# Four Strassen pairs of eight instead of three in gate and up, with the first weight sum made by accumulating DMA loads

## What is computed

```python
def _swiglu(h, w_gate, w_up, w_down):
    return (jax.nn.silu(h @ w_gate) * (h @ w_up)) @ w_down

x = x + _swiglu(_rmsnorm(x, ffn_norm[i]), ffn_w_gate[i], ffn_w_up[i], ffn_w_down[i])
```

## Time and profile before

| | |
|---|---|
| median of 3 runs | 2114.09 us (2113.99 to 2115.06) |
| the profiled execution: time, span | 2114.07 us, 2112.3 us |
| granted TensorE clock, mean | 0.998 |
| busy share PE, DVE, ACT, POOL | 99%, 82%, 56%, 1% |
| share of the chain that ended last: PE, DVE | 97%, 2% |
| DMA | mean 190 GB/s, the loads' queue 59.3% of the 16 engines |

### The profile page before, as it was taken

The page is one execution under the profiler, slowest core; times in us unless marked ns, Lnnn a source line. Parts: engine busy times, 40 slices in busy tenths (PEclk is TensorE's granted clock), DMA queues, the critical chain, the costliest instruction groups (busy, mean ns, idle before and its releaser), DMA issues.

```text
span 2112.3 us, 27946 instructions
## 1 busy us (share of the span) xinstructions
PE 2095.8 (99%) x9741; PEld 1743.9 (83%) x9741; DVE 1728.6 (82%) x1965; ACT 1179.5 (56%) x1321; POOL 15.4 (1%) x14
## 2 busy tenths in 40 slices
PE   8999999999999999999999999999999999999999
PEld 7888878888888888888878888888888888888887
DVE  5887757999999997877788788569999999978776
ACT  5466555665666654455455555555656565545443
POOL 0001000000000000000000000000000000000000
PEclk9999999999999999999999999999999999999999
DMA  7545555665666566666656665656665666566664
GB/s 229 156 139 154 173 169 176 199 208 189 199 199 207 190 198 200 199 198 192 191 183 191 186 201 186 199 178 198 201 200 188 200 200 200 193 204 196 206 198 132
DMA packets 234765, 401.63 MB, mean 190 GB/s; under 512 B 15040, under 2 KB 56128, under 8 KB 234688
## 3 DMA queue, kind: packets, MB, share of 16 engines
q1 hardware_dynamic: 233824, 399.23, 59.3%
q10 hardware_dynamic: 864, 1.37, 0.2%
HBM read 398.45 MB, written 2.10 MB: 190 GB/s over the span
## 4 chain that ended last, share of the span: by engine, by line
PE 97%; DVE 2%; ACT 0%; issue 0%; DMA 0%; SPq 0%; ACTq 0%; DVEq 0%
PE ps L767 24%; PE ps L769 24%; PE ps L768 24%; PE ps L513 6%; PE ps L544 4%; PE ps L542 4%; PE ps L543 4%; PE ps L518 3%; PE ps L577 2%; DVE w_lo L1354 0%; PE ps L695 0%; PE ps L633 0%; PE ps L704 0%; PE ps L685 0%; DMA res<-in_x 0%
## 5 line engine op out<-in xcount | busy, mean ns | idle before, releaser
L986 ACT ACTIVATE w_hi<-stage 128x1024 fp32r<-128x1024 f32 x748 | 782.0, 1057 | 755.4 <-PE ps L769 343.9
L1354 DVE TENSOR_TENSOR w_lo<-stage,w_hi 128x1024 fp32r<-128x1024 f32 x748 | 893.6, 1220 | 224.5 <-ACT w_hi L986 218.3
L767 PE MATMUL ps<-w_hi,xs 128*128 128x512 f32 x1254 | 491.0, 392 | 2.6 <-DVE w_lo L1354 2.6
L769 PE MATMUL ps<-w_hi,xs 128*128 128x512 f32 x1254 | 488.7, 390 | 0.0
L768 PE MATMUL ps<-w_lo,xs 128*128 128x512 f32 x1254 | 488.4, 389 | 0.0
L767 PEld LDWEIGHTS ps<-w_hi,xs 128*128 128x128 f32 x1254 | 235.7, 188 | 51.0 <-issue 3.0
L769 PEld LDWEIGHTS ps<-w_hi,xs 128*128 128x128 f32 x1254 | 235.6, 188 | 49.3
L768 PEld LDWEIGHTS ps<-w_lo,xs 128*128 128x128 f32 x1254 | 235.8, 188 | 48.1
L767 PE MATMUL ps<-w_hi,hs 128*128 128x512 f32 x584 | 227.6, 390 | 0.0
L769 PE MATMUL ps<-w_hi,hs 128*128 128x512 f32 x584 | 227.2, 389 | 0.0
L768 PE MATMUL ps<-w_lo,hs 128*128 128x512 f32 x584 | 227.2, 389 | 0.0
(11 more groups left out here) (209 smaller groups left out, 2480.9 us busy)
## 6 DMA issues: line engine op xcount, KB each, us to landing
stage<-in_w_gate SPq DMA_DIRECT2D x176, 512.0 KB, 3.7
stage<-in_w_up SPq DMA_DIRECT2D x176, 512.0 KB, 4.3
stage<-in_w_down SPq DMA_DIRECT2D x176, 512.0 KB, 4.5
stage<-in_conv_w_in SPq DMA_DIRECT2D x96, 512.0 KB, 4.3
stage<-in_attn_w_in SPq DMA_DIRECT2D x48, 512.0 KB, 3.7
stage<-in_attn_w_out SPq DMA_DIRECT2D x32, 512.0 KB, 5.2
stage<-in_conv_w_out SPq DMA_DIRECT2D x32, 512.0 KB, 4.8
stage<-in_attn_w_in SPq DMA_DIRECT2D x32, 256.0 KB, 3.2
```

Of the source, the lines that this page charges most:

```text
L767: pe.matmul(ps[:, bank, :], hi, b_hi, start=start, stop=False)
L769: return pe.matmul(ps[:, bank, :], lo, b_hi, start=False, stop=stop)
L986: nc.scalar.activation(w_hi[:, j % RING, :], stage[:, at, :], ACT.Copy).then_inc(hi_done, 1)
L1354: tt(w_lo[:, p, :], stage[:, stage_at(first + j), :], f32(w_hi[:, p, :]), ALU.subtract).then_inc(lo_done, 1)
```

## The change

- Gate and up have four mixed pairs in ten of the eleven units, 2, 3, 5 and 6; the last unit has 2 and 5. Pairs 2 and 3 and pairs 5 and 6 are neighbours. `sx` has four places.
- The signs of the scheme are turned so that the first sum of weights is b11 + b12. GpSimd makes it: a DMA from HBM that adds b11 (128 x 512, 256 KB) onto b12 in the odd slot in `stage` (`add_b11`), after that slot's load has landed and after the last such DMA has landed. The semaphore is `u1_added`. This holds for all mixed pairs, those of `down` and of the convolution too.
- `mix_weights` is two operations: one on 128 x 512 and one on 128 x 1024 that makes the other two sums with a repeated second operand. It waits for `t_ready` of the last pair (`t_raw` read), not for `t_used`.
- `mixed_high` and `mixed_low` are two operations each, 512 and 1024 columns. The wait for TensorE stands on ScalarE: the first copy waits for P6 of the last mixed pair, the second for P7.
- The convolution's third forms are made after slot 21 instead of slot 11.
- `P7` and `P5` change sign, in `take_mixed` and in the forms.

```diff
-        MIXED_PAIRS = (2, 4, 6)
-        LAST_MIXED = (2, 6)
-        FORM_PLACE = {4: 0, 2: 1, 6: 2}
+        MIXED_PAIRS = (2, 3, 5, 6)
+        LAST_MIXED = (2, 5)
+        FORM_PLACE = {3: 0, 6: 1, 2: 2, 5: 3}
+        CONV_PLACE = {4: 0, 2: 1, 6: 2}
...
-                pe.wait_ge(t_ready, count + s + 1)
-                product(P6, mixed_operand(kp, s, 1), t_hi[:, 1, :], t_lo[:, 1, :], first, last)
-                product(P4, half(operand, k2, 1), t_hi[:, 2, :], t_lo[:, 2, :], False, False)
+                pe.wait_ge(t_ready, 2 * (count + s) + 1)
+                product(P6, mixed_operand(kp, s, 1), t_hi[:, 2, :], t_lo[:, 2, :], first, last).then_inc(t_used, 1)
+                pe.wait_ge(t_ready, 2 * (count + s) + 2)
+                product(P4, half(operand, k2, 1), t_hi[:, 1, :], t_lo[:, 1, :], False, False)
                 product(P7, mixed_operand(kp, s, 3), t_hi[:, 0, :], t_lo[:, 0, :], first, last).then_inc(t_used, 1)
...
-                        act.wait_ge(t_first, after_first)
+                        act.wait_ge(u1_added, 16 * after_first)
...
             def mixed_high(count):
 
-                act.wait_ge(t_step, 3 * count + 3)
-                nc.scalar.activation(t_hi[:, :, :], t_raw[:, :, :], ACT.Copy).then_inc(t_high, 1)
+                act.wait_ge(t_step, 2 * count + 1)
+                if not isinstance(count, int) or count:
+                    act.wait_ge(t_used, 2 * count - 1)
+                nc.scalar.activation(t_hi[:, 2, :], t_raw[:, 2, :], ACT.Copy).then_inc(t_high, 1)
+                act.wait_ge(t_step, 2 * count + 2)
+                if not isinstance(count, int) or count:
+                    act.wait_ge(t_used, 2 * count)
+                nc.scalar.activation(t_hi[:, 0:2, :], t_raw[:, 0:2, :], ACT.Copy).then_inc(t_high, 1)
...
-                for jj in (j, j + 1):
-                    dve.wait_ge(loaded[stage_at(first + jj)], landed(first + jj, 16, i))
+                dve.wait_ge(loaded[stage_at(first + j)], landed(first + j, 16, i))
+                dve.wait_ge(u1_added, 16 * (count + 1))
+                left = stage[:, stage_at(first + j), :].rearrange("p (k n) -> p k n", k=2)
+                u1, b22 = (stage[:, stage_at(first + j + 1), k * WIDE:(k + 1) * WIDE] for k in range(2))
                 if not isinstance(count, int) or count:
-                    dve.wait_ge(t_used, count)
-                b11, b21 = (stage[:, stage_at(first + j), k * WIDE:(k + 1) * WIDE] for k in range(2))
-                b12, b22 = (stage[:, stage_at(first + j + 1), k * WIDE:(k + 1) * WIDE] for k in range(2))
-                t3, t2, t4 = (t_raw[:, form, :] for form in range(3))
-                tt(t3, b22, b12, ALU.subtract).then_inc(t_step, 1)
-                tt(b12, b12, b11, ALU.subtract).then_inc(t_first, 1)
-                dve.wait_ge(t_first, count + 1)
-                tt(t2, b22, b12, ALU.subtract).then_inc(t_step, 1)
-                dve.wait_ge(t_step, 3 * count + 2)
-                tt(t4, b21, t2, ALU.subtract).then_inc(t_step, 1)
+                    dve.wait_ge(t_ready, 2 * count)
+                tt(t_raw[:, 2, :], u1, b22, ALU.subtract).then_inc(t_step, 1)
+                dve.wait_ge(t_step, 2 * count + 1)
+                tt(t_raw[:, 0:2, :], left, bcast(t_raw[:, 2, :], 2), ALU.subtract).then_inc(t_step, 1)
...
-                dve.wait_ge(t_high, count + 1)
-                tt(t_lo[:, :, :], t_raw[:, :, :], f32(t_hi[:, :, :]), ALU.subtract).then_inc(t_ready, 1)
+                dve.wait_ge(t_high, 2 * count + 1)
+                tt(t_lo[:, 2, :], t_raw[:, 2, :], f32(t_hi[:, 2, :]), ALU.subtract).then_inc(t_ready, 1)
+                dve.wait_ge(t_high, 2 * count + 2)
+                tt(t_lo[:, 0:2, :], t_raw[:, 0:2, :], f32(t_hi[:, 0:2, :]), ALU.subtract).then_inc(t_ready, 1)
...
-                forms = merged({at: [lambda s=s: mix_conv(s, CONV_FORMS[s])] for s, at in enumerate((7, 9, 11))},
+                forms = merged({at: [lambda s=s: mix_conv(s, CONV_FORMS[s])] for s, at in enumerate((7, 9, 21))},
...
+            def add_b11(n, j, loop_slots, i, b11, count):
+
+                at = stage_at(n + j)
+                if not isinstance(count, int) or count:
+                    pool.wait_ge(u1_added, 16 * count)
+                pool.wait_ge(loaded[at], landed(n + j, loop_slots, i))
+                pool.dma_start(stage[:, at, 0:WIDE], b11, accum_op=ALU.add).then_inc(u1_added, 16)
```

More of the change, by code:

```diff
@@ L216, in trunk @@
         mixed_hi = sem("mixed_hi")
+        mixed_read = sem("mixed_read")
         t_step = sem("t_step")
-        t_first = sem("t_first")
+        u1_added = sem("u1_added")
         t_high = sem("t_high")
@@ L1186, in norm_steps @@
                 steps = {4: [lambda: res_square(q, j)], 6: [lambda: forms_high(q, j)]}
-                if j:
-                    steps = merged(steps, {7: [lambda: mixed_x_high(q, j)]})
+                forms = [lambda kp=kp: mixed_x_high(q, kp) for kp in MIXED_BY_CHUNK[j]]
+                steps = merged(steps, {8 if j == 3 else 7: forms})
                 return steps if j < 3 else merged(steps, {9: [lambda: take_root(q)]})
@@ L1321, in conv @@
             def conv(before):
-                forms = {at: [lambda s=s: conv_forms_high(s, CONV_FORMS[s])] for s, at in enumerate((8, 10, 12))}
+                forms = {at: [lambda s=s: conv_forms_high(s, CONV_FORMS[s])] for s, at in enumerate((8, 10, 22))}
                 before = merged(before, {10: [lambda: act.wait_ge(rs_ready, 2)]}, forms)
@@ L1635, in _, with add_in @@
             last_head_steps = head_steps(KV - 1, (1, 1, 1, 5, 5, 7))
[L1638 to L1640 removed]
+            def add_in(dst, bank, src, count, op=ALU.add):
+                tt(dst, ps[:, bank, :], src, op).then_inc(evicted, 1)
                 dve.wait_ge(evicted, count)
             def take_mixed(unit, count, at):
[L1645 removed]
+                dve.wait_ge(t_used, 2 * count)
                 dve.wait_ge(p1_taken, unit + 1)
@@ L1935, in _, with ffn, unit, down @@
                 cos_products(g)
+            def add_b11(n, j, loop_slots, i, b11, count):
[4 more added lines that the diff above has]
+                pool.dma_start(stage[:, at, 0:WIDE], b11, accum_op=ALU.add).then_inc(u1_added, 16)
+            def ffn(layer, first):
+                def unit(i):
+                    for s, kp in enumerate(mixed_of(i)):
+                        k1 = slice(2 * kp * P, (2 * kp + 1) * P)
+                        add_b11(first, 2 * kp + 1, 16, i, w_gate[layer][k1, :][:, bass.ds(WIDE * i, WIDE)],
+                                LAYER_MIXED * layer + FFN_MIXED * i + s)
+                unit(0)
+                with pool.Fori(1, BLOCKS - 1) as i:
+                    unit(i)
+                unit(BLOCKS - 1)
+            def down(layer, first):
+                for u in range(2):
+                    for s, kp in enumerate(DN_PAIRS):
+                        k1 = slice(2 * kp * P, (2 * kp + 1) * P)
+                        add_b11(first + FT * u, 2 * kp + 1, 0, 0, w_down[layer][k1, 2 * WIDE * u:2 * WIDE * u + WIDE],
+                                LAYER_MIXED * layer + ALL_FFN_MIXED + DN_MIXED * u + s)
+            ffn(0, S_GU0)
+            down(0, S_DN0)
+            for i in range(CONV_UNITS):
+                for s, kp in enumerate(CONV_PAIRS[i]):
+                    k1 = slice(2 * kp * P, (2 * kp + 1) * P)
+                    add_b11(S_CV + 24 * i, 2 * kp + 1, 0, 0, conv_w_in[k1, D + WIDE * i:D + WIDE * (i + 1)],
+                            conv_mixed(i) + s)
+            ffn(1, S_GU1)
+            down(1, S_DN1)
 def shape_constants():
```

66 lines of the change are left out of this document (38 added, 28 removed).

## The result

| | before | with the change |
|---|---|---|
| median of 5 runs, us | 2113.99 (2113.27 to 2115.06) | 2122.49 (2121.82 to 2123.03) |
| span of the profiled execution, us | 2112.3 | 2121.1 |
| granted TensorE clock, mean | 0.998 | 1.000 |
| matmuls | 9741 | 9681 |
| DMA, mean GB/s | 190 | 204 |

The ratio is 1.004, with a 95% interval of 1.0029 to 1.0051. The forecast was 2124.0 us.

The account below looks back on a forecast made before the run. TensorE was taken to bound gate and up, with VectorE close behind. Gains of 13.6 + 4.35 = 18 us against 28 us of waits turned 2114 into 2124 us, range 2100 to 2140.

Parts of the forecast that it names:

- Matmuls removed, 13.6 us: Gate and up: ten units per layer save 3 matmuls each, 13.6 us, all on TensorE's path.
- The wait at the unit's start: Gate and up: TensorE waits 0.85 us for `take_gate` at ten unit starts per layer, 0.4 after the first unit.
- The wait at slot 6: Gate and up, behind pair 2: TensorE waits 0.4 us for slot 6's low part in units 1 to 9 per layer.
- The first unit, 2.3: First gate and up unit of a layer: TensorE waits 2.3 us at slot 12.
- A unit, 42.9: Gate and up: a unit takes 41.69 + 0.4 + 0.85 = 42.9 us, against 42.37 in the kernel before.
- VectorE over 95% busy: Sign in the changed profile: VectorE is over 95% busy in the gate and up stretches.
- The convolution, 4.35: Convolution's first unit: the pause before slot 12 (2.78 us) and the lower clock (1.57) go, gaining 4.35 us.
- That short pauses leave the clock up: TensorE: short waits do not lower its clock, taken from an attention stretch with 1.56 us idle at clock 1.00.
- Accumulating DMAs, nothing on the path: Mixed pairs' first sums: the DMAs take 5 us at most, have 11.5, and cost nothing on the path.
- GpSimd holds up VectorE: Rival, chance 0.10: issuing a DMA slows VectorE once per unit, 1.22 x 20 = 24 us, giving 2148 us.
- Nothing waits for `u1_added`: Sign: the prediction is wrong if anything waits for `u1_added`, the accumulating DMAs' semaphore.
- The faster rival, 2101 us: Rival, chance 0.22: the unit-start wait goes, slot 6 is ready too; 2101 us with the first units' wait, 2096 without.

Follow-up runs that it names:

- the run without it: Changed kernel with only VectorE's order altered: a neighbouring mixed pair's even slot has its low part ahead of its sums; 2117.77 us, ratio 1.0017.
- the three-pair kernel: Changed kernel with its mixed pairs put back to 2, 4 and 6 (last unit 2 and 4), all else kept; 2109.64 us, ratio 0.9978.
- two runs: Changed kernel with the convolution's third forms back at slots 11 and 12, 2123.43 us; kernel before with them moved to 21 and 22, 2110.88 us.

## Why the prediction was right, point by point

- **Matmuls removed, 13.6 us: right.** The count fell by 60.
- **The wait at the unit's start, 0.85 at nine starts and 0.4 at the first: right in place and chain, one start too many.** It is 0.89 to 0.94 us, at eight starts per layer, and 0.1 at the first. The step that failed put the loop's table load in front of every unit; the last unit is outside the loop and has none. Reordering ScalarE alone took most of the wait away.
- **The wait at slot 6, 0.4: right in place, too large.** Its own gaps give 0.26, the run without it 0.23.
- **The first unit, 2.3: right in sum, partly wrong in place.** TensorE's pauses there are gaps of 0.51, then 0.57 with 0.35, then 1.70 with 0.31, that is 0.28, 0.46 and 1.55 us over the usual spacing, 2.3 in all. The prediction put all of it at slot 12, so the sum came out right by some luck.
- **A unit, 42.9: 42.94.** The start was a little dearer than 0.85 and slot 6 cheaper than 0.4; the two errors cancel.
- **VectorE over 95% busy: not quite.** It is busy 395.53 of 423 us, 94%, and 40.53 of 42.93 in one unit.
- **The convolution, 4.35: right.** The pause is gone, the three-pair kernel shows 4.4 us, and two runs took it apart into the move, the sums and the clock. That short pauses leave the clock up was taken from the earlier trace rows, whose 1.56 us of idle time are in fact two pauses, 1.39 and 0.18; the runs here bear it out.
- **Accumulating DMAs, nothing on the path: right, with the landing time taken too short.** I took 5 us at most; the median of the gate's 84 is 5.4, that of all 115 is 5.5, and the longest took 8.4. The Trainium skill, page "DMA: Bandwidth & Descriptors", section "Anatomy of one DMA — SWDGE (gpsimd) path", would give an estimate of 2.6 us; the trace does not agree: it took twice that. This DMA adds to what it finds and runs beside many loads; which of the two costs the time no run separates.
- **GpSimd holds up VectorE: did not happen.** GpSimd spends 0.88 us on each issue, and VectorE's operations beside it keep their 1.22 us (mean 1221 ns over 748). The Trainium skill, page "SBUF — State Buffer", section "Who interferes with whom", infers that writing descriptors does not block such operations; the trace agrees.
- **Nothing waits for `u1_added`: right in effect.** The trace names such a DMA as what ended VectorE's idle time seven times (2.4 us in all) and ScalarE's four times (6.7 us), so taken by the word this sign of being wrong came up. But the idle time there is what the same places have without it: 0.34 us at VectorE's first sum, as behind `hid` (3.8 us in 11), and 1.66 at ScalarE's copies, as where TensorE is named (400.31). In the unit of the first of them the DMA had landed by 397.17, when GpSimd issued the next, 3.7 us before the sum at 400.86. They cost nothing that can be seen.

The sum by the markers of the first layer: the first unit takes 2.02 us more (2.3 + 0.4 - 0.68 was forecast), the ten after it 4.03 (forecast 9 x (0.85 + 0.4 - 0.68) = 5.1, one start too many). The second layer's take 1.97 and 4.22, and the convolution 4.42 less: 7.8 in all. The spans differ by 8.8; the rest, 1.05, stands ahead of the first layer's gate and up (358.42 against 357.37). It is spread between executions: the same marker stands at 357.30 in the run with later DMAs and at 358.55 in the kernel before with the forms moved, with the same work ahead of it as in the changed kernel and the kernel before. Without it the change costs 7.8 us where 10 were forecast. The two starts too many (2 x 0.85) and the first starts, 0.1 instead of 0.4, are that difference; the medians, 8.5 apart, came nearer to the forecast by luck.

The faster rival, 2101 us, named the right condition: with the table load off the chain the 0.85 is gone, as the last unit of each layer shows. It was wrong that slot 6 is then ready too. ScalarE's new order removed the first wait alone (2107.86 us), and the second needed an edit of its own (2103.08 us).

## What to carry to other kernels

When an engine's work comes near to the whole time of its stage (here 41.1 of 41.7 us by the prediction), its sum of work no longer says whether it fits: write out the chain from the last event that releases it to the event that the bounding engine waits for, with every operation that merely stands in between. An operation in such a chain that nobody needs there (here two copies and one low part) is worth up to its whole length in every unit; here moving them cost nothing. A saving that loses should be tried with the order mended before it is given up: the fourth pair lost 13 us as it came and gained 6.6 once two list positions had changed.

## What the runs showed of the hardware

- A pause of 1.11 or 0.84 us of idle TensorE left the granted clock at its upper level (1.00 in the 5 us around it), and so did one of 1.31 us in the changed kernel's first unit (1.00 from 384 to 390 us); after 2.62 us the next eight matmuls ran at the lower one (0.78 and 0.88).
- An accumulating DMA of 256 KB from GpSimd lands 5.4 us after its issue by median (the gate's 84; all 115: 5.5, 4.1 to 8.4), longer than the 512 KB loads from SyncE of the same kernel (4.1 for the gate's). GpSimd is busy 0.88 us with the issue.
- SyncE's loads took a little longer beside them: those of the up weights 4.7 us, against 4.3 in the kernel before and 4.1 in the changed kernel without these DMAs.
- A table load of 1.28 us stands on ScalarE at the top of a hardware loop's body in every pass, and the copy behind it starts 0.02 us after its end (472.62 to 473.92); the unrolled copy of the same unit has none.
